# Picking the first expert pair's token rows with TensorE in a two-layer decoder trunk with a routed mixture of experts

## Chip, cores and metric

The kernel is one program on one core of a Trainium2 chip. The metric is the device time of one execution in microseconds (us); smaller is better. All engine times below come from one profiled execution of the kernel before the change.

## What is computed

A residual stream of 272 tokens (16 learned meta tokens ahead of 256 real ones, 1024 features, float32) goes through two layers. Each layer has a mixer (an mLSTM in layer 0, forgetting attention in layer 1, where the meta tokens are dropped) and behind it a mixture of experts, which is the part that the change touches:

```python
def hier_moe(h, w_group, b_group, w_router, b_router, w_gate, w_up, w_down):
    gl = x @ w_group + b_group                     # 4 groups
    top_g = argmax(gl);  p_g = softmax(gl)[top_g]
    el_g = (x @ w_router + b_router)[group top_g]  # 4 experts of that group
    top_v, top_i = top_k(el_g, 2)
    p_e = softmax(top_v) * p_g
    gates = one_hot(eidx) * p_e                    # 16 experts, 2 in use per token
    for grp in range(4):                           # dense in the reference
        act = silu(x @ w_gate) * (x @ w_up) * gates
        y += act @ w_down
    return y
```

with D_MODEL = 1024, 16 experts, an expert width of 256, and 272 tokens in layer 0, 256 in layer 1.

## The kernel before

The code is written per engine: each of SyncE (SP), GpSimd (POOL), ScalarE (ACT), VectorE (DVE) and TensorE (PE) has its own hand-written instruction order, and engines meet at counting semaphores. `in_layer(name, l, n)` is the wait for the n-th increment of a semaphore in layer l.

The expert stage doesn't compute all experts for all tokens. DVE's `route` (from L826) finds two experts for each token and gives each (token, expert) a slot: expert e has 64 slots, two experts form a pair b of 128 slots, and there are 8 pairs. The slot numbers of a token's two experts stand in `tok4[:, 0:2, t]`, for token tiles t = 0, 1 (128 tokens each) and, in layer 0 alone, t = 2 (the 16 meta tokens). The normalised rows of the stream stand in SBUF in `tok` (L589, ACT), and ACT also writes them to DRAM as `xs` (L593).

For pair b the kernel needs the rows of its 128 slots, transposed, in `xgT[b % 2]`. Before the change all eight pairs get them the same way:

- DVE's `one_hot` (L866) and `one_hot_late` (L909) write bf16 one-hot masks `sel` (token x slot).
- PE's `rows_of_slots` (L1369) multiplies them with the token numbers `tcol`, one output column per pair; DVE's `row_of_slot` (L823) makes integers `idx` of it.
- POOL's indirect DMA (L456) gathers the 128 rows of `xs` into `xg[b % 3]`.
- PE's `rows_to_cols` (L1402) transposes them, in two halves of four blocks through `bank[0]`; DVE's `x_evac` (L917) takes the first half out, ACT's `xgT_evac` (L623) the second, both times the norm's gains.

Then for each pair PE runs `gate_up` (L1420, 16 float32 products of 128x512, two column halves of the array at a time), ACT and DVE form silu(gate) x up, PE's `act_tr` (L1427) transposes it, `down` (L1444) and `combine` (L1459 in layer 0, L1463 in layer 1) follow one pair later. A float32 product shows as two MATMUL records, a transpose and a bf16 product as one.

The mixing weights reach the token axis by `tokens_to_rows` (L1382), a copy `row4` (L968), `spread_rows` (L1389) and ACT's `rows_spread` (L615). `keep_busy` (L1349) runs products whose result nobody reads.

Weights stream through a ring of 12 slots of 1 MB (`RING`), filled by SP in a fixed order (L304): six of a pair (gate, up, gate, up, down, down). A gate or up slot is free when the `gate_up` of two pairs earlier is done, a down slot when that pair's `down` is done, and SP waits in order. The first two pairs' weights are loaded while the layer's output projection still runs.

PE's order around the first pair before the change: slot counting, `keep_busy(8)`, `rows_of_slots` of block 0, `keep_busy(18)`, both halves of `rows_to_cols(0)`, `rows_of_slots` of blocks 1 to 3, `tokens_to_rows`, `gate_up(0)`, `spread_rows`, `rows_of_slots` of blocks 4 to 7, `rows_to_cols(1, 0)`, `act_tr(0)`, `rows_to_cols(1, 1)`, `gate_up(1)`, `down(0)`.

Of the kernel before, what the change touches and what calls it, by code (L numbers as in the profile page):

```python
# [11 lines left out]
P = 128  # L12
# [28 lines left out]
def build(nc, io, out):  # L41
    ctx = ExitStack()
    with ctx:
# [56 lines left out]
        comb = big[:, NY * D:NY * D + NPAIR * NT].rearrange("p (b t) -> p b t", t=NT)  # L100
        sel = big[:, 0:6 * 256].bitcast(BF16).rearrange("p (c t s) -> p c t s", c=2, t=3)
# [136 lines left out]
        def wait_bank(pe, kind, ph, j):  # L238
            if before(kind, ph) + j >= 2:
# [7 lines left out]
                  "sel_ready": 5, "idx_mm": 3, "tok4_ready": 1, "row4_mm": 1, "row4_ready": 1, "at_done": 8,  # L247
                  "at_read": 8, "comb_ready": 8, "c_done": 64, "x_in0": 48, "x_in1": 48, "x_in2": 32}
# [131 lines left out]
        def _(pool):  # L380
# [68 lines left out]
            def moe(l):  # L449
                tiles, n, off = tiles_of(l)  # L450
                pool.wait_ge(*in_layer("xs_written", l, 16 * len(tiles)))
                for b in range(NPAIR):
                    pool.wait_ge(*in_layer("idx_ready", l, (1, 2, 2, 2, 3)[min(b, 4)]))
                    if b >= NXG:
                        pool.wait_ge(*in_layer("tx_done", l, 2 * (b - NXG) + 2))
                    pool.indirect_dma_start(  # L456
                        out=xg[b % NXG], out_offset=None, in_=xs[l],
                        in_offset=bass.IndirectOffsetOnAxis(ap=idx[:, b:b + 1], axis=0)) \
                        .then_inc(sem(f"x_in{b % NXG}"), 16)
                pool.wait_ge(*in_layer("ktot_ready", l, 1))  # L460
# [23 lines left out]
        def _(act):  # L484
# [86 lines left out]
            def moe(l):  # L571
# [12 lines left out]
                def rows_out(t, rows):  # L584
# [6 lines left out]
                    link(ins)  # L591
                    r0 = (META, META + P, 0)[t] - off
# [46 lines left out]
                xgT_evac(0)  # L639
# [72 lines left out]
        def _(dve):  # L712
# [113 lines left out]
            def route(l):  # L826
# [8 lines left out]
                t4n, t4bn, dnn, gmn, pgn, exn, dvn = [a[:, 0:nt, :] for a in (t4, t4b, dn, gm, pg, ex, dv)]  # L835
# [43 lines left out]
                one_hot(0, 0, P)  # L879
# [5 lines left out]
                row_of_slot(l, 0, 0, 1, 1)  # L885
                link(dve.tensor_reduce(v12[:, :, 0:nt, 0], t16[:, :, 0:nt, :], AX.X, ALU.add))
                dve.tensor_tensor(dvn, v12[:, 1, 0:nt, :], v12[:, 0, 0:nt, :], ALU.subtract).then_inc(sem("v_sub"), 1)
                one_hot(P, P, 2 * P)
                one_hot(3 * P, 3 * P, P)
# [10 lines left out]
            def moe(l):  # L900
# [64 lines left out]
                x_evac(0)  # L965
                row_of_slot(l, 1, 1, 4, 2)
# [9 lines left out]
                for b in range(NPAIR):  # L976
# [5 lines left out]
                    else:  # L982
                        row_of_slot(l, 3, 4, 8, 3)
                    if b + 1 < NPAIR:
                        x_evac(b + 1)
                    actT_evac(b)
# [189 lines left out]
        def _(pe):  # L1176
# [145 lines left out]
            def moe(l):  # L1322
# [69 lines left out]
                def rows_to_cols(b, half):  # L1392
                    if half == 0:
                        pe.wait_ge(*in_layer(f"x_in{b % NXG}", l, 16 * (b // NXG + 1)))
                        if b >= 1:
                            pe.wait_ge(*in_layer("xT_read", l, b))
                        else:
                            pe.wait_ge(*in_layer("idx_ready", l, 1))
# [6 lines left out]
                def gate_up(b):  # L1405
# [4 lines left out]
                    else:  # L1410
                        pe.wait_ge(*in_layer("idx_ready", l, 2))
# [4 lines left out]
                    for q in range(KB):  # L1416
                        for par in (0, 1):
# [48 lines left out]

                rows_to_cols(0, 0)
                rows_to_cols(0, 1)
                rows_of_slots(3, 1, (1, 2, 3))
                tokens_to_rows()  # L1470
                for b in range(NPAIR):
                    gate_up(b)
                    if b == 0:
                        spread_rows()
                        rows_of_slots(5, 3, (4, 5, 6, 7))
                    if b >= 1:
                        down(b - 1)
                    if b + 1 < NPAIR:
                        rows_to_cols(b + 1, 0)
                    act_tr(b)  # L1480
                    if b >= 1:
                        combine(b - 1, 0)
                    if b + 1 < NPAIR:
# [192 lines left out]
```

## Time and profile before

| | us |
|---|---|
| three timed runs | 687.52, 689.30, 689.37 |
| their median | 689.3 |
| the profiled execution, its own time | 687.83 |
| its span, first to last instruction | 686.1 |
| PE busy | 642.8 (94%) |
| DVE busy | 204.6 (30%) |
| ACT busy | 143.9 (21%) |
| POOL busy | 30.5 (4%) |
| mean granted TensorE clock | 0.972 |

The rows are read as follows. The chain of work that ended last names at each step the instruction that the next one waited for. The timeline lists instructions of each engine in order of time; a neighbouring few of one line are merged (xN), and the time in brackets is idle time before them with what ended it. The views by stretch give busy time, the granted TensorE clock (1.00 is 2.4 GHz, 0.50 is 1.2 GHz) and the busy share of the DMA engines. Durations overlap where an engine pipelines: six instructions of 0.27 us can take 1.25 us together.

### The profile page before, as it was taken

The page shows a single profiled execution, that of the slowest core. Times are in us where ns is not written, and L with a number is a line of the kernel's source. Part 1 is how long each engine was busy: PE and PEld are TensorE (multiplying, and loading weights), DVE is VectorE, ACT ScalarE, POOL GpSimd, SP SyncE. Part 2 cuts the span into 40 slices and gives each one's busy share as a digit, 9 for nine tenths or more (in the row PEclk, how much of TensorE's full clock was granted, in tenths as well). Part 3 has the DMA queues.
Part 4 walks back from the last instruction along what each step waited for, and adds up shares of the span by engine and source line. Part 5 has one row for each costly group of instructions (what it writes and reads, how often), then busy time and mean ns, then how long its engine had stood idle before and what let it go on. Part 6 is the DMA issues. An engine that isn't in the chain of part 4 may idle for free.

```text
span 686.1 us, 7900 instructions
## 1 busy us (share of the span) xinstructions
PE 642.8 (94%) x3052; PEld 399.4 (58%) x3052; DVE 204.6 (30%) x588; ACT 143.9 (21%) x396; POOL 30.5 (4%) x60
## 2 busy tenths in 40 slices
PE   6889999999998999999988999999999889999994
PEld 3577877777674355544446777777677433334331
DVE  2423112222153244444362333333312422112211
ACT  1112012332141011111032333333213211111110
POOL 5000000000002000000001000000000300000000
PEclk9998999999999899999999999999999889999998
DMA  9996232113334599999995504132334376999921
GB/s 289 278 279 216 69 148 88 64 62 122 123 137 140 249 374 415 419 420 416 350 349 177 184 20 166 62 124 67 118 123 155 116 312 274 409 422 419 421 106 63
DMA packets 59114, 150.05 MB, mean 219 GB/s; under 512 B 10082, under 2 KB 42914, under 8 KB 46786
## 3 DMA queue, kind: packets, MB, share of 16 engines
q1 hardware_dynamic: 55554, 136.71, 53.8%
q0 software_dynamic: 2912, 10.64, 4.4%
q10 hardware_dynamic: 608, 2.16, 0.8%
q8 instruction: 26, 0.43, 0.2%
q14 instruction: 14, 0.11, 0.0%
HBM read 146.27 MB, written 3.23 MB: 218 GB/s over the span
## 4 chain that ended last, share of the span: by engine, by line
PE 82%; DMA 8%; ACT 3%; DVE 3%; issue 1%; SPq 1%; ACTq 0%; DVEq 0%
PE bank L1186 34%; PE bank L1420 15%; PE bank L1444 7%; DMA ring<-in_moe_w_up 6%; PE bank L1459 3%; PE bank L1463 3%; PE bank L1281 3%; PE bank L1402 2%; DMA qk_area<-xs,idx 1%; PE bank L1584 1%; PE bank L1195 1%; PE bank L1571 1%; PE bank L1213 1%; PE bank L1613 1%; ACT tok L589 1%
## 5 line engine op out<-in xcount | busy, mean ns | idle before, releaser
L1186 PE MATMUL bank<-xT,ring 128*128 128x272 f32 x640 | 156.8, 401 | 5.2 <-ACT qk_area L523 3.0
L1186 PEld LDWEIGHTS bank<-xT,ring 128*128 128x128 f32 x640 | 122.4, 194 | 32.3 <-issue 6.4
L1420 PE MATMUL bank<-ring,gate_area 128*64 128x512 f32 x512 | 120.8, 627 | 5.9 <-DMA ring<-in_moe_w_up 2.8
L1420 PEld LDWEIGHTS bank<-ring,gate_area 128*64 128x64 f32 x512 | 39.2, 144 | 81.5 <-issue 81.5
L1186 PE MATMUL bank<-tok,ring 128*128 128x272 f32 (+1 forms) x256 | 61.0, 391 | 0.6 <-DVE tok L1170 0.6
L1444 PE MATMUL bank<-ring,gate_area 128*64 128x512 f32 x256 | 57.9, 593 | 0.0
L1186 PEld LDWEIGHTS bank<-tok,ring 128*128 128x128 f32 x256 | 47.4, 190 | 13.5 <-issue 6.1
L936 DVE TENSOR_TENSOR qk_area<-qk_area,bank 128x256 f32<-128x256 f32 x16 | 6.7, 422 | 122.7 <-ACT qk_area L631 122.7
L1444 PEld LDWEIGHTS bank<-ring,gate_area 128*64 128x64 f32 x256 | 19.1, 137 | 35.6 <-issue 35.6
L456 POOL DMA_INDIRECT qk_area<-xs,idx x16 | 18.1, 1129 | 456.7 <-DMA xs<-tok 329.1
L631 ACT ACTIVATE qk_area<-bank 128x256 f32<-128x256 f32 x16 | 6.1, 384 | 131.9 <-PE bank L1420 131.9
L1459 PE MATMUL bank<-big 128*128 128x272 f32 x128 | 32.5, 399 | 1.2 <-DVE big L950 1.2
L1463 PE MATMUL bank<-big 128*128 128x512 f32 x64 | 30.6, 606 | 1.1 <-DVE big L950 1.1
L1402 PEld LDWEIGHTS bank<-ident,qk_area 128*128 128x128 f32 x128 | 18.0, 193 | 20.7 <-issue 12.6
L501 ACT ACTIVATE colT<-hT 128x272 f32<-128x272 f32 (+1 forms) x32 | 13.5, 426 | 76.0 <-DVE hT L818 59.0
L955 DVE TENSOR_TENSOR hT<-hT,bank 128x272 f32<-128x272 f32 x64 | 27.7, 436 | 5.0 <-PE bank L1459 4.1
L1186 PE MATMUL bank<-big,ring 128*128 128x256 f32 x128 | 28.9, 379 | 0.0
L623 ACT ACTIVATE gate_area<-bank,gains_x 128x128 f32<-128x128 f32 x64 | 18.3, 368 | 50.3 <-PE bank L1402 50.3
L1402 PE MATMUL bank<-ident,qk_area 128*128 128x128 f32 x128 | 22.4, 300 | 6.1 <-DMA qk_area<-xs,idx 3.6
L1459 PEld LDWEIGHTS bank<-big 128*128 128x128 f32 x128 | 23.2, 190 | 6.7 <-DVE big L950 2.2
L1186 PEld LDWEIGHTS bank<-big,ring 128*128 128x128 f32 x128 | 24.3, 190 | 3.5
L950 DVE COPY big<-bank 128x512 f32<-128x512 f32 x16 | 11.1, 691 | 45.7 <-PE bank L1444 45.7
(243 smaller groups left out, 593.0 us busy)
## 6 DMA issues: line engine op xcount, KB each, us to landing
ring<-in_moe_w_gate SPq DMA_DIRECT2D x32, 1024.0 KB, 12.3
ring<-in_moe_w_up SPq DMA_DIRECT2D x32, 1024.0 KB, 14.1
ring<-in_moe_w_down SPq DMA_DIRECT2D x32, 1024.0 KB, 7.5
ring<-in_m_w_in SPq DMA_DIRECT2D x12, 1024.0 KB, 11.7
ring<-in_kv_w SPq DMA_DIRECT2D x8, 1024.0 KB, 11.9
ring<-in_m_w_out SPq DMA_DIRECT2D x4, 1024.0 KB, 11.0
ring<-in_f_w_q SPq DMA_DIRECT2D x4, 1024.0 KB, 12.3
ring<-in_f_w_o SPq DMA_DIRECT2D x4, 1024.0 KB, 5.1
```

The costliest lines, as they stand in the source:

```text
L456: pool.indirect_dma_start(out=xg[b % NXG], out_offset=None, in_=xs[l], in_offset=bass.IndirectOffsetOnAxis(ap=idx[:, b:b + 1], axis=0)) \
L501: act.activation(colT[k % 2][:, 0:n], hT[:, k, c0:c0 + n], ACT.Square).then_inc(sem(f"sq_{name}"), 1)
L623: ins = act.activation(xgT[b % 2][:, q, :], bank[0][:, (q - 4) * P:(q - 3) * P], ACT.Copy, scale=gains_x[:, l, q:q + 1])
L950: dve.tensor_copy(yb[b % NY][:, 0:HALF], bank[2][:, :]).then_inc(sem("y_read0"), 1)
L955: dve.tensor_tensor(hT[:, i, :], hT[:, i, :], bank[4 + i % 4][:, 0:NT], ALU.add) \
L1186: ins = pe.matmul(bank[c % 2][:, 0:n], w[:, k, half * P:half * P + P], x[:, k, 0:n], start=(k == 0), stop=(k == KB - 1))
L1281: ins = pe.matmul(bank[b][:, q0:NT], lhs, wexp[0:kr, hd, c:c + NT - q0], start=(m == 0), stop=(m == 2), skip_group_check=True)
L1402: ins = pe.transpose(bank[0][:, i * P:(i + 1) * P], xg[b % NXG][:, 4 * half + i:D:KB], ident[:, :])
L1420: ins = pe.matmul(bank[1][s, :], xgT[b % 2][:, q, s], ring[:, r:r + 2, q * FE:(q + 1) * FE], start=(q == 0), stop=(q == KB - 1))
L1444: ins = pe.matmul(bank[2 + half][s, :], haT[b % 2][:, f, s], unit_down(us[par])[:, f, half * HALF:(half + 1) * HALF], start=(f == 0), stop ...
L1459: ins = pe.matmul(bank[4 + i % 4][:, 0:n], y[:, i * P:(i + 1) * P], comb[:, b, 0:n], start=True, stop=True)
L1463: ins = pe.matmul(bank[4 + i][:, :], comb[:, b, t * P:(t + 1) * P], y[:, half * HALF:(half + 1) * HALF], start=(b == 0), stop=(b == NPAIR ...
```

## The change

For the first pair no gather is made. DVE writes a float32 one-hot mask `sel0` of 128 slots, both experts of a token in one mask (one comparison per tile, then one comparison-and-add per tile). PE's `pick_rows` multiplies the rows in `tok` by it: for each of 8 feature blocks one float32 product per token tile, accumulated, 4 blocks into `bank[0]` and 4 into `bank[1]`. The result is the transposed rows. DVE's `first_evac` takes both halves out; ACT has no part in it. PE waits for `rows_in_sbuf` (the rows of all tiles written by ACT) and `sel0_ready`.

The rest is order:

- The slot's token numbers are worked out in parts: block 1 ahead of `gate_up(0)`, blocks 2 and 3 and `tokens_to_rows` in the middle of it (behind its fourth of eight steps), blocks 4 to 7 behind it. POOL gathers pair 1 after the first part, 2 and 3 after the second, the others after the third.
- `keep_busy(18)` is gone, `keep_busy(8)` is `keep_busy(10)`.
- The six small DVE operations on the mixing weights (`gate_weights`) are moved out of `route`, behind `first_evac` and the first `row_of_slot`.
- Behind `gate_up(0)` PE's order becomes `rows_to_cols(1, 0)`, `spread_rows`, `rows_to_cols(1, 1)`, `rows_of_slots` of blocks 4 to 7, `act_tr(0)`, `gate_up(1)`. On DVE `x_evac(1)` comes ahead of `row_of_slot` of the last blocks.

```diff
-                for b in range(NPAIR):
-                    pool.wait_ge(*in_layer("idx_ready", l, (1, 2, 2, 2, 3)[min(b, 4)]))
+                for b in range(1, NPAIR):
+                    pool.wait_ge(*in_layer("idx_ready", l, min(b // 2, 2) + 1))
...
                     link(ins)
+                    act.sem_inc(sem("rows_in_sbuf"), 1)
...
-                xgT_evac(0)
...
-                one_hot(0, 0, P)
+                for t, rows, _ in tiles:
+                    ins = dve.tensor_scalar(sel0[0:rows, t, :], iota_f[0:rows, 0:P], tok4[0:rows, 0, t:t + 1], None,
+                                            ALU.is_equal)
+                link(ins)
+                for t, rows, _ in tiles:
+                    ins = dve.scalar_tensor_tensor(sel0[0:rows, t, :], iota_f[0:rows, 0:P], tok4[0:rows, 1, t:t + 1],
+                                                   sel0[0:rows, t, :], ALU.is_equal, ALU.add)
+                ins.then_inc(sem("sel0_ready"), 1)
+                one_hot(P, P, P)
...
-                row_of_slot(l, 0, 0, 1, 1)
...
-                one_hot(P, P, 2 * P)
-                one_hot(3 * P, 3 * P, P)
+                one_hot(2 * P, 2 * P, 2 * P)
+            def gate_weights(l):
...
+                def first_evac(half):
+                    dve.wait_ge(*in_layer("tx_done", l, half + 1))
+                    q = slice(4 * half, 4 * half + 4)
+                    dve.tensor_tensor(xgT[0][:, q, :], bank[half][:, :].rearrange("p (q s) -> p q s", q=4),
+                                      gains_x[:, l, q].unsqueeze(2).to_broadcast([P, 4, P]), ALU.mult) \
+                        .then_inc(sem(("xT_read0", "xT_read")[half]), 1)
...
-                x_evac(0)
-                row_of_slot(l, 1, 1, 4, 2)
+                first_evac(0)
+                first_evac(1)
+                row_of_slot(l, 0, 1, 2, 1)
+                gate_weights(l)
+                row_of_slot(l, 0, 2, 4, 2)
...
-                keep_busy(8)
-                if l == 0:
-                    pe.wait_ge(*in_layer("xr_read", l, 1))
-                rows_of_slots(1, 0, (0,))
-                keep_busy(18)
+                keep_busy(10)
+                def pick_rows(half):
+                    for i in range(4):
+                        for m, (t, rows, _) in enumerate(tiles):
+                            ins = pe.matmul(bank[half][:, i * P:(i + 1) * P], tok[0:rows, t, 4 * half + i:D:KB],
+                                            sel0[0:rows, t, :], start=(m == 0), stop=(m == nt - 1))
+                    ins.then_inc(sem("tx_done"), 1)
...
                     for q in range(KB):
+                        if b == 0 and q == KB // 2:
+                            pe.wait_ge(*in_layer("idx_ready", l, 1))
+                            rows_of_slots(2, 0, (2, 3))
+                            tokens_to_rows()
...
-                rows_to_cols(0, 0)
-                rows_to_cols(0, 1)
-                rows_of_slots(3, 1, (1, 2, 3))
-                tokens_to_rows()
+                pe.wait_ge(*in_layer("rows_in_sbuf", l, nt))
+                pe.wait_ge(*in_layer("sel0_ready", l, 1))
+                pick_rows(0)
+                pick_rows(1)
+                pe.wait_ge(*in_layer("xT_read0", l, 1))
+                rows_of_slots(1, 0, (1,))
                 for b in range(NPAIR):
                     gate_up(b)
-                    if b == 0:
-                        spread_rows()
-                        rows_of_slots(5, 3, (4, 5, 6, 7))
                     if b >= 1:
                         down(b - 1)
                     if b + 1 < NPAIR:
                         rows_to_cols(b + 1, 0)
+                    if b == 0:
+                        spread_rows()
+                        rows_to_cols(1, 1)
+                        rows_of_slots(4, 3, (4, 5, 6, 7))
                     act_tr(b)
```

## Rows read from the trace of the kernel before

**Rows 1.** Page, the chain that ended last, shares of the span by engine

```profile
PE 82%; DMA 8%; ACT 3%; DVE 3%; issue 1%; SPq 1%; ACTq 0%; DVEq 0%
```

**Rows 2.** The chain in order of time: start us, us, what, both layers

```profile
203.03 4.70 DMA qk_area<-xs,idx
...
211.95 8.29 PE bank L1420 x32
...
228.02 8.82 PE bank L1420 x32
...
542.43 8.63 PE bank L1420 x32
...
556.79 9.97 PE bank L1420 x32
```

**Rows 3.** Timeline of ACT and DVE, layer 0: start us, us, engine, instruction

```profile
199.20 1.25 ACT L589 ACTIVATE tok<-bank,rs 16x512 f32<-16x512 f32 x2 [0.40 <-ACT tok L589]
...
199.66 0.26 DVE L878 TENSOR_REDUCE tok<-gate_area 128x6 f32<-128x96 f32 x1
199.96 1.25 DVE L866 TENSOR_SCALAR big<-iota_f,tok 128x128 bf16<-128x128 f32 x6
...
202.43 3.06 DVE L866 TENSOR_SCALAR big<-iota_f,tok 128x256 bf16<-128x256 f32 x12
...
208.52 0.69 DVE L917 TENSOR_TENSOR gate_area<-bank,gains_x 128x512 f32<-128x512 f32 x1 [1.94 <-PE bank L1402]
...
225.81 0.49 DVE L925 SCALAR_TENSOR_TENSOR gate_area<-gate_area,s_cols 128x272 f32<-128x272 f32 x1
```

**Rows 4.** Timeline of PE, layer 0, from the routing on, and a later gate

```profile
201.82 4.29 PE L1349 MATMUL bank<-ident,ones_f 128*128 128x128 f32 x36
...
207.77 0.71 PE L1402 MATMUL bank<-ident,qk_area 128*128 128x128 f32 x4 [1.66 <-DMA qk_area<-xs,idx]
...
209.81 1.50 PE L1369 MATMUL bank<-tcol,big 128*128 128x1 bf16 x18
...
211.25 0.70 PE L1382 MATMUL bank<-ident,tok 128*4 128x128 f32 x3
...
220.17 2.10 PE L1389 MATMUL bank<-colT,sel 4*128 4x272 f32 x8
...
222.20 1.99 PE L1369 MATMUL bank<-tcol,big 128*128 128x1 bf16 x24
...
293.20 7.09 PE L1420 MATMUL bank<-ring,gate_area 128*64 128x512 f32 x32 [0.91 <-DMA ring<-in_moe_w_up]
```

**Rows 5.** Timeline of PE and DVE, layer 1

```profile
529.85 2.03 PE L1349 MATMUL bank<-ident,ones_f 128*128 128x128 f32 x16
...
530.81 0.22 DVE L878 TENSOR_REDUCE tok<-gate_area 128x4 f32<-128x64 f32 x1
...
552.91 0.55 PE L1369 MATMUL bank<-tcol,big 128*128 128x1 bf16 x16
```

**Rows 6.** Line L1402: weight loads, duration ns min/median/max, first and last start

```profile
L1402 PEld LDWEIGHTS bank<-ident,qk_area x128: 185/190/231, 207.8 to 652.0; 128*128 128x128 f32 x128
```

**Rows 7.** Groups by shape, 201.7 to 206.2 us: busy us, mean ns, idle before

```profile
L1349 PEld LDWEIGHTS bank<-ident,ones_f 128*128 128x128 f32 x36 | 4.1, 192 | 0.0
```

**Rows 8.** Busy by stretch: us, PE busy (x), granted clock, DMA share, GB/s

```profile
211.00:214.60 3.60, 3.60 (x15) 0.53 0.18 40
...
224.70:228.00 3.30, 1.68 (x8) 0.50 0.98 412
...
556.80:562.60 5.80, 5.80 (x14) 0.50 1.02 425
```

**Rows 9.** SP's waits, 195 to 345: us in total, times, longest

```profile
SPq L304 <- PE bank L1444: 82.8, 6, 17.9
```

**Rows 10.** One steady pair: us, busy PE, PEld, DVE, ACT, POOL, clock, DMA

```profile
255.88:271.50 15.62, 15.62 (x76) 7.51 (x75) 6.72 (x15) 2.13 (x6) 0.94 (x1) 1.00 1.01 414
```

**Rows 11.** Line L456, the 16 gathers: time from issue to landing

```profile
DMA to landing us min/median/max: 4.6/6.4/10.2
```

More of the change, by code:

```diff
@@ L100, in build @@
         comb = big[:, NY * D:NY * D + NPAIR * NT].rearrange("p (b t) -> p b t", t=NT)
+        sel0 = big[:, 6 * 256:6 * 256 + 3 * P].rearrange("p (t s) -> p t s", t=3)
         sel = big[:, 0:6 * 256].bitcast(BF16).rearrange("p (c t s) -> p c t s", c=2, t=3)
@@ L246, in build @@
                   "act_ready": 8, "down_done": 8, "y_read0": 8, "y_read1": 8, "eall_ready": 1, "pos_mm": 1,
-                  "sel_ready": 5, "idx_mm": 3, "tok4_ready": 1, "row4_mm": 1, "row4_ready": 1, "at_done": 8,
-                  "at_read": 8, "comb_ready": 8, "c_done": 64, "x_in0": 48, "x_in1": 48, "x_in2": 32}
+                  "sel_ready": 4, "idx_mm": 3, "tok4_ready": 1, "row4_mm": 1, "row4_ready": 1, "at_done": 8,
+                  "at_read": 8, "comb_ready": 8, "c_done": 64, "sel0_ready": 1, "rows_in_sbuf": 3, "x_in0": 32, "x_in1": 48, "x_in2": 32}
         def in_layer(name, l, n):
@@ L834, in route @@
                 gl, el = lg[:, 0:nt, 0:NG], lg[:, 0:nt, NG:NG + NE]
-                t4n, t4bn, dnn, gmn, pgn, exn, dvn = [a[:, 0:nt, :] for a in (t4, t4b, dn, gm, pg, ex, dv)]
+                t4n, gmn, dvn = [a[:, 0:nt, :] for a in (t4, gm, dv)]
                 ogb = og[:, 0:nt, :].unsqueeze(3).to_broadcast(full)
@@ L884, in route @@
                 link(dve.tensor_tensor(t16[:, :, 0:nt, :], el.unsqueeze(1).to_broadcast(both), e12[:, :, 0:nt, :], ALU.mult))
-                row_of_slot(l, 0, 0, 1, 1)
                 link(dve.tensor_reduce(v12[:, :, 0:nt, 0], t16[:, :, 0:nt, :], AX.X, ALU.add))
                 dve.tensor_tensor(dvn, v12[:, 1, 0:nt, :], v12[:, 0, 0:nt, :], ALU.subtract).then_inc(sem("v_sub"), 1)
-                one_hot(P, P, 2 * P)
-                one_hot(3 * P, 3 * P, P)
+                one_hot(2 * P, 2 * P, 2 * P)
+            def gate_weights(l):
+                tiles, n, off = tiles_of(l)
+                nt = len(tiles)
+                t4bn, dnn, pgn, exn = [a[:, 0:nt, :] for a in (t4b, dn, pg, ex)]
                 dve.wait_ge(*in_layer("gl_exp", l, 1))
@@ L981, in moe @@
                         y_evac(b - 1)
-                    else:
-                        row_of_slot(l, 3, 4, 8, 3)
                     if b + 1 < NPAIR:
                         x_evac(b + 1)
+                    if b == 0:
+                        row_of_slot(l, 3, 4, 8, 3)
                     actT_evac(b)
@@ L1393, in rows_to_cols @@
                     if half == 0:
[L1394 to L1398, printed above, removed]
+                        pe.wait_ge(*in_layer(f"x_in{b % NXG}", l, 16 * (b // NXG + (b % NXG > 0))))
+                        pe.wait_ge(*in_layer("xT_read", l, b))
+                        if b == 1:
+                            pe.wait_ge(*in_layer("idx_ready", l, 2))
                     else:
@@ L1409, in gate_up @@
                         pe.wait_ge(*in_layer("at_read", l, b))
-                    else:
-                        pe.wait_ge(*in_layer("idx_ready", l, 2))
                     us = [expert_units(l, b, par) for par in (0, 1)]
@@ L1479, in moe @@
                         rows_to_cols(b + 1, 0)
+                    if b == 0:
+                        spread_rows()
+                        rows_to_cols(1, 1)
+                        rows_of_slots(4, 3, (4, 5, 6, 7))
                     act_tr(b)
@@ L1482, in moe @@
                         combine(b - 1, 0)
-                    if b + 1 < NPAIR:
+                    if 1 <= b < NPAIR - 1:
                         rows_to_cols(b + 1, 1)
```

## The prediction, made blind

> **What bounds the kernel now.** I read the chain that ended last first: it is TensorE for 82% of the span and DMA for 8% [rows 1]. Anything that the change gives must therefore be found on PE's own path or in what PE waits for. The chain in order of time then says where the first expert pair stands: in layer 0 it leaves PE for the gather (203.03, 4.70 us) and comes back at the transposes, and the first gate stage runs from 211.95 for 8.29 us, the second from 228.02 for 8.82 us; in layer 1 they start at 542.43 and 556.79 and last 8.63 and 9.97 us [rows 2]. A later one, from 293.20, lasts 7.09 us [rows 4]. So each layer holds two things: a detour (mask, token numbers, gather, transposes, two evacuations) and early gate stages that are slower than the later ones. The view by stretch names the reason for the second: the clock was at 0.50 to 0.53, that is at 1.2 GHz, in 211 to 214.6, in 224.7 to 228, and in 556.8 to 562.6 [rows 8]. Before each fall PE had run transposes and one-column products and been idle in between; it came back while gate products ran.
>
> Behind the second gate stage everything is tied to PE. SP's longest waits, six of them, are for L1444, the down stage [rows 9], so the weight stream starts again from there. In a steady pair PE is busy all of its 15.62 us and the DMA engines are too (1.01, 414 GB/s) [rows 10]. Both shift together if the first `down` comes earlier.
>
> **Layer 0, up to the first gate stage.** The slots are known at 199.66 + 0.26 = 199.92 [rows 3]. The mask `sel0` takes three comparisons and three comparison-adds of 128 columns. Six comparisons take 1.25 us with 0.27 for the first alone, so 0.20 each behind it [rows 3]; for the comparison-add no row has this size: a 272-column one takes 0.49 [rows 3], a comparison 0.27, and I take 0.30 and 0.22 for each further one. Sum 0.67 + 0.74 + 0.05 for the link = 1.46, so `sel0` is ready at 201.4. ACT's last row is there at 200.45 [rows 3] and doesn't decide; PE's ten idle products (20 records at 0.12) end near 201.2.
>
> `pick_rows` is the new cost, and its price is the main unknown. It is 2 x 4 x 3 = 24 float32 products, 48 records. The nearest row is `keep_busy`: 36 records of the same moving shape in 4.29 us, 0.119 each [rows 4]. The other bound is the transposes from the same kind of strided operand: 4 records in 0.71; with the last one's 0.28 taken off, 0.14 to 0.15 between starts [rows 4]. I take 0.12, as a load over the stride lasts as long (median 190 ns) as one of `ones_f` (mean 192) [rows 6, 7]; 0.147 would add 80 x 0.027 = 2.2 us over both layers. So 48 x 0.12 + 0.16 = 5.9 us, end at 207.4. One evacuation (0.69 [rows 3]) is hidden beside the second half, DVE being through its masks at about 205.6 (201.4 + 1.25 + 1.15 for five small steps + 3.06 - 1.25 for the wide ones [rows 3]); the other stands on the path. The first gate stage starts at 207.4 + 0.05 + 0.69 = 208.2, against 211.9: **3.7 us** sooner. The six one-column products of block 1 (0.5 us at 1.50/18 [rows 4]) lie beside that evacuation.
>
> The stride has a rule against it. The Trainium skill, SBUF — State Buffer, in its note on cachelines, says that reads which step to a new 16-byte line each time pay a penalty; `tok[..., i:D:8]` steps 32 bytes. The trace doesn't agree (190 beside 192 ns). The page gives no figure; by the rule the sum would go toward its upper bound.
>
> **Layer 0, first gate stage to second.** Two pieces move into the stage: 12 one-column products, 12 x 1.50/18 = 1.0, and `tokens_to_rows`, 0.63 [rows 4]. At full clock the stage is 7.1 + 1.6 = 8.7 and ends at 216.9 (220.2 before). The added wait there, for `idx_ready`, holds nothing: DVE writes that column at 208.4, four steps take until 211.8. Behind it: `rows_to_cols(1,0)` 0.7, `spread_rows` 2.0, second half 0.7, 24 one-column products 2.0 [rows 4], `act_tr` 0.5 and its copy 0.5, in all 6.4, so `gate_up(1)` starts at 223.3. ACT's evacuation of pair 1 (1.14, some 220.6 to 221.8) is now beside the one-column products, where it used to be last. Against 228.02: **4.7 us**.
>
> The masks for blocks 4 to 7 start on DVE only when `row4` is copied, at 214.1, and take 3.2, so they end at 217.3; their reader comes at 220.3. The six `gate_weights` steps (1.2 us) lie between 208.5 and 211.9, where DVE has nothing else. POOL's first gather is issued near 208.7 and lands 4.7 to 10.2 us later [rows 2, 11]; it is wanted at 216.9, so there are 8.2 us for it, and it is alone on the queue. The later gathers keep their order.
>
> **Layer 1** has two tiles. Slots at 531.03 [rows 5], `sel0` at 532.1; PE's idle products, from 529.85 [rows 5], end at 532.3 and decide. 32 records: 3.84 + 0.16, end at 536.3; evacuation, start at 537.1 against 542.43: 5.3 us. The stage takes 7.05 + 0.35 + 0.5 = 7.9 (the one-column products are 0.55/16 each here [rows 5]); then 0.7 + 2.0 + 0.7 + 0.55 + 0.5 + 0.5 = 5.0. Second gate stage at 550.1 against 556.79: **6.7 us**.
>
> **The clock in the second gate stage.** It cost 8.82 - 7.09 = 1.73 us in layer 0 and 9.97 - 7.09 = 2.88 in layer 1 [rows 2, 4]. After the change the quiet stretch behind `spread_rows` is 3.6 us instead of 5.8, and 2.1 instead of 3.8. Real products fill the place where gather waits stood, so the first gate stage should run at full clock (already in the sums). For the second I can't say: bounds for what is left are 0 and the old cost; I take 1.3 in each, so the change gives back 1.73 + 2.88 - 2.6 = **2.0 us**.
>
> Here one rule bears. In the Trainium skill, TensorE: Matmul & The Clock Gate, Part 4, transposes are said not to count as busy for the clock. The low clock from 224.7 and at 556.8 [rows 8] came behind one-column products and transposes, which agrees. By that rule the quiet stretch lasts up to the gate stage and the clock still falls; if transposes did count, it might not, which is the rival of 672.4 below.
>
> **Sum:** 4.7 + 6.7 + 2.0 = 13.4. From the profiled execution, 687.8 - 13.4 = 674.4; from the median of 689.3 it would be 675.9. I take 675.0.
>
> **Rivals.**
> - *The weight stream decides.* It starts again first at the end of `gate_up(0)`, which moves by only 3.3 and 5.9 us. If PE later waits for weights as before (0.91 us ahead of the stage at 293.20 [rows 4], and alike in layer 1) and that wait grows by the rest, 687.8 - 9.2 = 678.6. For it speaks the full DMA share; against it that the six long waits are for `down` [rows 9], which moves in full.
> - *The gather of pair 1 lands late.* At 10.2 us it comes 2.0 us late in layer 0 and, issued at 537.6 and wanted at 545.0, 2.8 late in layer 1: 674.4 + 4.8 = 679.2. Against it: a single gather took 4.70.
> - *The clock falls before the picks*, as PE waits for `sel0`. Each record then takes twice as long: 80 x 0.12 = 9.6 more, 684.0. The idle time is only 0.3 us, far less than what lay ahead of the falls [rows 8].
> - *The clock never falls:* 674.4 - 2.6 = 671.8 from this execution, 672.4 from the middle of both starts.
> - *Slower.* The picks don't pipeline because each product loads its own strided weights: load and product behind one another, 0.19 + 0.28 = 0.47 per record. 80 x 0.35 = 28 more, 702. It decides from 0.12 + 13.4/80 = 0.29 per record. `keep_busy` has loads of 0.192 and still starts a record each 0.119 [rows 4, 7].
> - *It doesn't do what it says:* the wait goes elsewhere in front of `gate_up(0)`, 687.8. DVE would have to be the late one by 4 us; its queue holds no such thing.
>
> **How the numbers follow.** The forecast 0.60, weight stream 0.12, late gather 0.10, clock low in the picks 0.06, clock never low 0.08, slower 0.02, no effect 0.02. The forecast's own ends are 672.5 (old clock cost gone in one layer) and 679 (0.147 per record, no clock gain). The range 671.0 to 680.5 takes in all but about 0.15. A difference of 0.3% (2 us) is about what a measurement of this kernel can tell from none; by these cases faster 0.96, same 0.02, slower 0.02.
>
> **What would show it.** Right: no idle PE at L1402 for a gather in front of the first gate stage; the picks 48 and 32 records in 5.9 and 4.0 us at clock 1.00; the first gate stage starting 8.3 us behind the slot reduction in layer 0 and 6.3 in layer 1; the gap between the first two gate stages 6.4 and 5.0; 15.6 us per pair behind it as before. Wrong: picks spaced over 0.15 us, a clock of 0.50 within them, a new wait for `qk_area<-xs,idx` before pair 1, DVE still at its masks when the first half is picked, or PE's waits for weights up by more than 1 us.

## The result, and the profile after

The changed kernel takes 692.3 us (median of 14 runs, 690.2 to 697.1) where the kernel before takes 689.2 (14 runs, 685.9 to 690.6): ratio 1.005, 95% interval 1.0034 to 1.0067. It is slower by half a per cent, and the interval leaves out 1, where 675.0 us and a range of 671.0 to 680.5 had been forecast. The profiled execution took 692.3 us with a span of 690.6, 4.5 us more than the 686.1 of before.

**The chain.** By engine, from the page of the kernel after, to be read beside [rows 1]:

```profile
PE 86%; DMA 6%; DVE 3%; ACT 2%; issue 1%; SPq 1%; DVEq 0%; ACTq 0%
```

The gather is off the chain, as the change intends (DMA 6% for 8%), and PE has taken more than its place. The chain in order of time (start us, us, what), layer 0 and then layer 1, says with what:

```profile
201.63 16.00 PE bank L1404 x48
218.46 4.99 PE bank L1450 x16
223.45 0.96 PE bank L1394 x12
...
224.83 3.58 PE bank L1450 x16
...
235.13 8.62 PE bank L1450 x32
...
540.03 7.86 PE bank L1404 x32
...
548.72 5.35 PE bank L1450 x16
554.59 3.58 PE bank L1450 x16
...
562.78 8.64 PE bank L1450 x32
```

L1404 is `pick_rows`, L1450 is `gate_up`. The picks take 16.00 and 7.86 us, forecast at 5.9 and 4.0. The first gate stage starts at 218.46 where it had started at 211.95 [rows 2].

**The picks themselves.** One line's instructions (duration ns min/median/max, first and last start, shapes), kernel after, beside [rows 6, 7] with their 190 and 192:

```profile
L1404 PEld LDWEIGHTS bank<-big,tok x80: 307/335/340, 201.6 to 547.4; 128*128 128x128 f32 x64, 16*128 16x128 f32 x16
L1404 PE MATMUL bank<-big,tok x80: 396/439/607, 201.6 to 547.5; 128*128 128x128 f32 x64, 16*128 16x128 f32 x16
```

Each weight load takes 335 ns. And the clock, by stretch (us, PE busy (x), granted clock, DMA share, GB/s), kernel after:

```profile
201.63:204.00 2.37, 2.37 (x9) 1.00 0.07 19
204.00:205.00 1.00, 1.00 (x4) 0.57 0.00 0
205.00:217.60 12.60, 12.60 (x39) 0.50 0.00 0
218.46:221.00 2.54, 2.54 (x6) 0.50 0.00 0
540.03:547.50 7.47, 7.47 (x32) 1.00 0.11 42
549.00:552.00 3.00, 3.00 (x8) 0.50 0.25 70
```

In layer 0 the clock falls to its lower level (1.2 GHz) in the midst of the picks, while PE shows no idle time, and stays there into the first gate stage. (In front of them it had been idle for 0.45 us, waiting for `sel0`.) In layer 1 the picks run at 1.00 from end to end, 7.86/32 = 0.25 us each, and the clock falls just behind them.

**Where the 4.5 us are.** At the end of layer 0's second gate stage the kernel is 243.75 - 236.84 = 6.9 us behind. PE's wait for a weight, 0.91 us before [rows 4], is 1.67, which with the rest of layer 0 makes layer 1's share start 7.7 late (slots known at 538.50 against 530.81 [rows 5]). Timeline of PE, kernel after, that stage (the row stops where the view was cut off):

```profile
300.87 4.51 PE L1450 MATMUL bank<-ring,gate_area 128*64 128x512 f32 x20 [1.67 <-DMA ring<-in_moe_w_up]
```

Timeline of DVE, kernel after, where layer 1's slots are known:

```profile
538.50 0.22 DVE L879 TENSOR_REDUCE tok<-gate_area 128x4 f32<-128x64 f32 x1
```

Layer 1 gives 3.0 back: its second gate stage ends at 571.42, which less 7.7 is 563.7, where it was 566.8 before. 6.9 + 0.8 - 3.0 is 4.7; the 4.5 of the spans leave 0.2 for what comes behind. So layer 1, with two tiles and an undisturbed clock in its picks, is a gain even at the double price, and layer 0 is a loss.

### The profile page after: what moved, and what is told of

Read it like the earlier page. It is cut to its first block, busy times and chain, and to the rows that moved or that the text cites. A ratio compares the mean times of both kernels' runs of the same rounds, so it can differ in the third digit from the quotient of the medians.

```text
span 690.6 us, 7878 instructions
## 1 busy us (share of the span) xinstructions
PE 653.8 (95%) x3042; PEld 409.5 (59%) x3042; DVE 206.3 (30%) x590; ACT 141.6 (21%) x388; POOL 28.6 (4%) x58
## 4 chain that ended last, share of the span: by engine, by line
PE 86%; DMA 6%; DVE 3%; ACT 2%; issue 1%; SPq 1%; DVEq 0%; ACTq 0%
PE bank L1211 33%; PE bank L1450 15%; PE bank L1474 7%; DMA ring<-in_moe_w_up 6%; PE bank L1404 3%; PE bank L1489 3%; PE bank L1493 3%; PE bank L1306 3%; PE bank L1430 2%; PE bank L1617 1%; PE bank L1220 1%; PE bank L1604 1%; PE bank L1238 1%; PE bank L1646 1%; PE bank L1342 1%
## 5 line engine op out<-in xcount | busy, mean ns | idle before, releaser
L1450 PE MATMUL bank<-ring,gate_area 128*64 128x512 f32 x512 | 120.0, 621 | 5.8 <-DMA ring<-in_moe_w_up 3.4
L1450 PEld LDWEIGHTS bank<-ring,gate_area 128*64 128x64 f32 x512 | 38.9, 143 | 78.8 <-issue 78.8
L457 POOL DMA_INDIRECT qk_area<-xs,idx x14 | 16.2, 1155 | 462.6 <-DVE idx L824 371.6
L1430 PEld LDWEIGHTS bank<-ident,qk_area 128*128 128x128 f32 x112 | 15.5, 192 | 15.4 <-issue 14.9
L1404 PE MATMUL bank<-big,tok 128*128 128x128 f32 (+1 forms) x80 | 23.9, 453 | 0.5 <-DVE big L886 0.5
L625 ACT ACTIVATE gate_area<-bank,gains_x 128x128 f32<-128x128 f32 x56 | 16.0, 368 | 32.6 <-PE bank L1430 32.6
```

What stands on the lines that cost most here:

```text
L457: pool.indirect_dma_start(out=xg[b % NXG], out_offset=None, in_=xs[l], in_offset=bass.IndirectOffsetOnAxis(ap=idx[:, b:b + 1], axis=0)) \
L625: ins = act.activation(xgT[b % 2][:, q, :], bank[0][:, (q - 4) * P:(q - 3) * P], ACT.Copy, scale=gains_x[:, l, q:q + 1])
L1404: ins = pe.matmul(bank[half][:, i * P:(i + 1) * P], tok[0:rows, t, 4 * half + i:D:KB], sel0[0:rows, t, :], start=(m == 0), stop=(m == nt - 1))
L1430: ins = pe.transpose(bank[0][:, i * P:(i + 1) * P], xg[b % NXG][:, 4 * half + i:D:KB], ident[:, :])
L1450: ins = pe.matmul(bank[1][s, :], xgT[b % 2][:, q, s], ring[:, r:r + 2, q * FE:(q + 1) * FE], start=(q == 0), stop=(q == KB - 1))
```

## The experiments

My first theory was that the stride of the picks' weights costs the time: `tok[..., i:D:8]` takes every eighth float32 of a row. Its rivals: float32 products with new weights in each cost that much in any layout; the clock alone; the new order behind the picks. Each ratio below is to the kernel before, timed together with the experiment. Where a time is that of a single execution, it proves little by itself, and only durations within it are compared.

**1. The same picks without the stride.**

```diff
-    ins = pe.matmul(bank[half][:, i * P:(i + 1) * P], tok[0:rows, t, 4 * half + i:D:KB],
+    ins = pe.matmul(bank[half][:, i * P:(i + 1) * P], tok[0:rows, t, (4 * half + i) * P:(4 * half + i + 1) * P],
```

> The kernel after with one thing changed: the weights that the picks load are 128 neighbouring features of a row instead of every eighth one. The experts of the first pair then get features in another order, so this kernel computes something else for that pair; its amount of work is the same. Theory A (the stride makes each weight load long): loads back from 335 to about 190 ns, layer 1's 32 records from 7.9 to about 3.9 us, layer 0's 48 records from 16.0 to about 5.8 us with the clock at 1.00 throughout, and the whole at about 678 us. Theory B (a float32 product with these two operands is slow whatever the stride): loads stay at 335 ns and layer 1 at 7.9 us, the whole stays at 692 us. Theory C (only the fallen clock costs): layer 1, where the clock stayed at 1.00, doesn't change.

681.2 us, ratio 0.9863 (0.9816 to 0.9911), where the changed kernel has 1.005. The line of the picks, the chain and the clock in them, this kernel:

```profile
L1404 PEld LDWEIGHTS bank<-big,tok x80: 181/192/192, 202.3 to 538.0; 128*128 128x128 f32 x64, 16*128 16x128 f32 x16
```

```profile
202.31 8.48 PE bank L1404 x48
211.62 5.35 PE bank L1450 x16
...
534.62 3.81 PE bank L1404 x32
```

```profile
202.31:210.60 8.29, 8.29 (x48) 1.00 0.02 4
```

The edit changes one access pattern and nothing else, and takes 11 us away. Layer 1's picks cost 3.81 us, 0.119 a record, the forecast's own price; the clock held within the picks in both layers. Layer 0's still cost 8.48 for 48 records, 0.177 each, so something is left there: see 5. Behind them the first half of the gate stage still took 5.35 us in layer 0, where it takes 3.65 at full clock.

**2. At which stride it begins.** The same line with every second and every fourth feature (8 and 16 bytes between elements) instead of every eighth (32 bytes).

> As before but every second feature (8 bytes between elements). The rule of 16-byte lines in the Trainium skill (SBUF - State Buffer, note on cachelines) has two elements in a line and no or a small penalty: loads near 190 ns. If instead any step costs: 335 ns.

> As before but every fourth feature (16 bytes between elements, one element to a line). By the rule of 16-byte lines the full penalty of the kernel after, 335 ns per load; if the cost goes with the number of bytes stepped over, about halfway between 190 and 335 ns.

679.0 and 695.1 us in a single execution each. The picks' loads with every second, then with every fourth feature:

```profile
L1404 PEld LDWEIGHTS bank<-big,tok x80: 187/196/197, 200.4 to 533.6; 128*128 128x128 f32 x64, 16*128 16x128 f32 x16
```

```profile
L1404 PEld LDWEIGHTS bank<-big,tok x80: 303/330/330, 204.2 to 550.2; 128*128 128x128 f32 x64, 16*128 16x128 f32 x16
```

4, 8, 16 and 32 bytes give 192, 196, 330 and 335 ns: a step between 8 and 16 bytes, and nearly no slope at either side. So the price doesn't grow with the distance; it fits a price for loads of which no two elements share 16 bytes. (Steps of 12 bytes and other starts within the 16 were not run.) The Trainium skill, SBUF — State Buffer, asks in Specifications (TRN2) for two or more hits to each 16-byte line; the runs agree with that for these loads. It is the rule that the prediction had set aside.

**3. Product or transpose.** The row I had set it aside on was a transpose's. The kernel before, with only the first pair's eight turnings written as float32 products with the identity, on the same gathered buffer with the same stride:

```diff
-    ins = pe.transpose(bank[0][:, i * P:(i + 1) * P], xg[b % NXG][:, 4 * half + i:D:KB], ident[:, :])
+    src = xg[b % NXG][:, 4 * half + i:D:KB]
+    if b == 0:
+        ins = pe.matmul(bank[0][:, i * P:(i + 1) * P], src, ident[:, :], start=True, stop=True)
+    else:
+        ins = pe.transpose(bank[0][:, i * P:(i + 1) * P], src, ident[:, :])
```

> The kernel before with one thing changed: the first pair's gathered rows are turned by float32 products with the identity instead of transposes, from the same gathered buffer with the same stride of eight. If float32 products load their weights slower over a stride and transposes don't, the loads go from 190 to 335 ns here too, 16 records instead of 8. If the rows' own buffer in the kernel after is the cause, they stay at 190 ns. The whole: 1 to 4 us slower than before at most.

692.4 us in a single execution. Groups by shape in 200 to 213 us (busy us, mean ns, idle before), this kernel:

```profile
L1404 PEld LDWEIGHTS bank<-ident,qk_area 128*128 128x128 f32 x16 | 4.0, 334 | 2.7 <-DMA qk_area<-xs,idx 1.8 <-DVE gate_area L917 1.0
```

334 ns as a product, 190 as a transpose [rows 6], same buffer, same stride, same shape. The row of the transposes was a true one and said nothing of a product's loads.

**4. The layout made contiguous with the right output.** ACT writes the normalised rows block by block, and the picks, the transposes and the later use of `xg` read 128 neighbours.

```diff
+    by_block = tok[0:rows, t, :].rearrange("r (k p) -> r p k", k=KB)
...
-    ins = act.activation(tok[0:rows, t, half * HALF:(half + 1) * HALF], b[0:rows, :], ACT.Copy,
+    ins = act.activation(by_block[:, half * 64:(half + 1) * 64, :],
+                         b[0:rows, :].rearrange("r (p k) -> r p k", k=KB), ACT.Copy,
```

> The kernel after, computing what the reference asks, with the feature order changed: ACT writes each normalised row block by block (feature 8p + i to column 128i + p), so every weight load of the picks and of the transposes of the gathered rows reads neighbouring elements. Stride theory: the picks as with stride 1, 48 records in about 8.5 us and 32 in 3.8, the whole near 681 us. Against it: ACT's copies write 512 bytes apart; if they slow down from 0.64 to 1 us each, the mask waits for rows and the whole loses 2 to 3 us, 683.

> The kernel before with the blocked feature order alone, first pair still gathered. Transposes already loaded in 190 ns over the stride, so the order alone should be worth nothing: 689 us, within 0.3%. If it were worth several us, the gain of after_blocked over before would not be the picks'.

The changed kernel with it: 688.1 us, ratio 0.9977 (0.9955 to 0.9999). The kernel before with the layout alone: 695.1, ratio 1.008 (1.0048 to 1.0112), which I had put at nothing. ACT's copies (timeline of ACT) in the kernel before and then in the second of these:

```profile
195.84 1.27 ACT L589 ACTIVATE tok<-bank,rs 128x512 f32<-128x512 f32 x2
```

```profile
194.36 2.06 ACT L590 ACTIVATE tok<-bank,rs 128x512 f32<-128x512 f32 x2
```

The price has moved to the writer: 0.8 us for each tile, in front of the gather or the picks. In the kernel before with this layout that is not all of the loss: in layer 1 the write of the rows to DRAM, on which the gather waits, lands 4.53 us after its issue where it took 2.65, and no run says why. In the changed kernel with it, PE waits for the copies, and the clock falls in the picks though their loads are cheap. Groups by shape in 198 to 220 us, and by stretch:

```profile
L1406 PE MATMUL bank<-big,tok 128*128 128x128 f32 x32 | 8.9, 427 | 1.8 <-ACTq L595 1.8
L1406 PE MATMUL bank<-big,tok 16*128 16x128 f32 x16 | 6.0, 475 | 0.0
```

```profile
205.00:217.50 12.50, 12.50 (x44) 0.50 0.00 0
```

The 48 records take 13.9 us here and 8.5 in 1, with the same operands: the low clock alone costs 5.4. In layer 1 they take 3.84. So the fall in the picks isn't the stride's doing alone: it came with cheap loads behind an idle time of 1.8 us, and with dear loads behind one of 0.5.

**5. What is left in layer 0: the 16 meta rows.** There each block of picks is three products, over 128, 128 and 16 rows. Two theories: a record over 16 rows is dear by itself; or the change between loads of 128 and of 16 rows is. Kernel 1 again, the third product over 128 rows of tile 0:

```diff
-    ins = pe.matmul(bank[half][:, i * P:(i + 1) * P], tok[0:rows, t, (4 * half + i) * P:(4 * half + i + 1) * P],
-                    sel0[0:rows, t, :], start=(m == 0), stop=(m == nt - 1))
+    u = t % 2
+    ins = pe.matmul(bank[half][:, i * P:(i + 1) * P], tok[:, u, (4 * half + i) * P:(4 * half + i + 1) * P],
+                    sel0[:, u, :], start=(m == 0), stop=(m == nt - 1))
```

> As pick_stride1, and in layer 0 the third product of each block reads tile 0 with 128 rows again instead of the meta tokens' 16 rows; so it computes something else for the first pair, with the same number of records. Theory E (records over 16 rows cost about twice those over 128): layer 0's 48 records take 5.8 us instead of 8.5. If three accumulated products cost that in themselves: 8.5 us as before.

676.9 us in a single execution. Timeline of PE, this kernel:

```profile
200.36 5.60 PE L1405 MATMUL bank<-big,tok 128*128 128x128 f32 x48 [0.45 <-DVE big L886]
```

More rows in the array, and 2.9 us less. To tell the two theories apart I took kernel 4 and put all 16-row products of a half behind the others. This kernel doesn't compute what the reference asks for the first pair; the amount of work is the same.

```diff
-    for i in range(4):
-        for m, (t, rows, _) in enumerate(tiles):
+    blocks = [(i, m) for i in range(4) for m in range(min(nt, 2))] + [(i, 2) for i in range(4) if nt == 3]
+    for i, m in blocks:
+        t, rows, _ = tiles[m]
...
```

> As after_blocked, and in layer 0 the products over the 16 rows of meta tokens come last in each half instead of every third. With stride 1 layer 0's picks took 0.177 us a record where layer 1's took 0.119. Theory D (changing between 128 and 16 rows of weights breaks the overlap of load and product): layer 0's 48 records drop from 8.5 toward 5.8 us, the whole by 2 to 3 us to about 678.5. Theory E (a load over 16 rows is slow wherever it stands): no change.

681.7 us, ratio 0.9876 (0.9841 to 0.9911); the picks took 9.38 us, not the 5.8 that grouping would give if the change of height were the cost. I first read that as the end of that theory, and it was a misreading: the low clock fell into this stretch too. By stretch, and the loads of the last group on their own (timeline of weight loads), this kernel:

```profile
205.00:210.00 5.00, 5.00 (x23) 0.50 0.00 0
211.40:212.20 0.80, 0.80 (x7) 1.00 0.00 0
```

```profile
211.32 0.96 PEld L1407 LDWEIGHTS bank<-big,tok 16*128 16x128 f32 x8 [0.22 <-issue]
```

Back at full clock, eight 16-row loads stand in 0.96 us, 0.12 each: as cheap as 128 rows. Another kernel separates the two at full clock. It is kernel 1 with every second block in reverse order (128, 128, 16, then 16, 128, 128), so that the sums hold and the height changes 8 times instead of 15:

```diff
-    for m, (t, rows, _) in enumerate(tiles):
+    for m, (t, rows, _) in enumerate(tiles[::(1, -1)[i % 2]]):
```

> The kernel after with the picks at stride 1 (each block takes 128 neighbouring features instead of every eighth, so the columns of the first pair's rows stand in another order, as in pick_stride1), and every second block takes its tiles in reverse (128, 128, 16, then 16, 128, 128 rows), so that the 48 records of layer 0 change between 128 and 16 rows 8 times instead of 15. At stride 1 and full clock a record starts 0.112 us behind the one before; the records at a change cost some 0.1 more each, and the 48 took 8.48 us where all of 128 rows took 5.60. Theory CHANGE (what costs is the change of height between one product's weights and the next's, 2.88 us / 15 = 0.19 each): the picks of layer 0 take 5.6 + 8 x 0.19 = 7.1 us, layer 1's stay at 3.81, the 16-row records in the middle of a run of four start 0.112 apart, and the time is about 1.4 us below that of pick_stride1, 679.9. Theory HEIGHT (a record over 16 rows is dearer by itself, 0.18 more for each of the 16): the picks stay at 8.5 us and the time at 681.2.

679.2 us, ratio 0.9837 (0.9778 to 0.9895). Timeline of PE, this kernel:

```profile
204.28 7.14 PE L1404 MATMUL bank<-big,tok 128*128 128x128 f32 x48 [0.45 <-DVE big L886]
```

7.14 us where the change of height gives 7.1 and a price of the height itself 8.5. The starts of the records within one and a half blocks show it singly; ns from each record to the next, 16-row records in brackets:

```
every eighth feature, clock 1.00 (after)           239 238 331 [340 326] 339
every eighth feature, clock 0.50 (after)           238 242 378 [399 370] 400
neighbours, clock 1.00 (pick_stride1)              112 112 205 [213 200] 213 112
neighbours, clock 1.00 (pick_stride1_turned)       112 112 205 [213 112 111 200] 214 111
neighbours, clock 0.50 (after_blocked)             213 214 350 [375 347] 374 213
```

At full clock each change of height costs two records some 0.09 to 0.10 us more, at the lower one 0.13 to 0.16. And a record over the stride takes 238 to 242 ns at either clock: the lower clock costs it nothing by itself, only at the changes.

**6. The rest of the change without the picks.** Pair 0 gathered and transposed as before, with its token numbers and `keep_busy` of before; the parts of the other token numbers, the moved weight steps and the new order kept. One thing is neither before nor after: PE waits for block 1's numbers (`idx_ready`) in front of the first gate stage, where the changed kernel waits for them in its middle.

```diff
-    pe.wait_ge(*in_layer("sel0_ready", l, 1))
-    pick_rows(0)
-    pick_rows(1)
+    rows_to_cols(0, 0)
+    rows_to_cols(0, 1)
...
+    pe.wait_ge(*in_layer("idx_ready", l, 2))
```

> The kernel after with the picks undone: the first pair's rows are gathered and transposed as before, all the rest is in the new order (block 1's numbers ahead of the first gate stage, blocks 2 and 3 and the mixing weights' transposes inside it, the new sequence behind it). From the traces the gap between the first two gate stages shrank from 7.8 to 6.7 and from 5.7 to 4.6 us: so 2 us faster than before, 687, if the order brings what the traces suggest; the moved pieces lengthen the first gate stage by what they left out in front of it, nothing either way. Rival: it brings up to 4 us, as fewer one-column products stand in front of the first gate stage.

690.1 us, ratio 1.0021 (0.9998 to 1.0044): not the 687 that I had put, and no gain. Timeline of PE, this kernel:

```profile
211.83 5.88 PE L1450 MATMUL bank<-ring,gate_area 128*64 128x512 f32 x16 [0.98 <-DVE idx L825]
...
229.17 3.68 PE L1450 MATMUL bank<-ring,gate_area 128*64 128x512 f32 x8 [0.67 <-issue]
```

The first half of the gate stage takes 5.88 us, at a clock of 0.61, where before it took 4.8 (16 records from 211.88 to 216.64), and the inserts lengthen the stage by 1.3. The gap behind it shrinks from 7.8 to 6.5 us, which doesn't pay for that: the second gate stage starts 2.3 us later than before, both measured from the masks' start. Of these 2.3 us about 1.0 is this kernel's own wait for `idx` in front of the stage, which the changed kernel doesn't have. So the run shows no gain of the order behind a gather; what the order is worth behind quick picks was not run by itself.

**7. Select first, then turn.** The mask as the stationary operand and 512 contiguous features moving; ACT copies each half to `xg[0]`, and eight strided transposes turn it. Transposes don't pay for the stride, and neither do products over neighbours. Two idle products (`keep_busy(2)`) stand between the selection and the transposes.

```diff
-    for i in range(4):
-        for m, (t, rows, _) in enumerate(tiles):
-            ins = pe.matmul(bank[half][:, i * P:(i + 1) * P], tok[0:rows, t, 4 * half + i:D:KB],
-                            sel0[0:rows, t, :], start=(m == 0), stop=(m == nt - 1))
+    for m, (t, rows, _) in enumerate(tiles):
+        ins = pe.matmul(bank[half][:, :], sel0[0:rows, t, :], tok[0:rows, t, half * HALF:(half + 1) * HALF],
+                        start=(m == 0), stop=(m == nt - 1))
...
+    act.activation(xg[0][:, half * HALF:(half + 1) * HALF], bank[half][:, :], ACT.Copy)
...
+    ins = pe.transpose(bank[half][:, i * P:(i + 1) * P], xg[0][:, 4 * half + i:D:KB], ident[:, :])
```

> The kernel after, computing what the reference asks, with the first pair's rows selected the other way round: the mask is the stationary operand (contiguous) and the rows the moving one, 512 features at a time (6 products in layer 0, 4 in layer 1, 0.44 us each at full clock), ACT copies both halves to the gather's buffer, and 8 transposes over the stride (190 ns loads) turn them as before. If the picks' price in the kernel after is the strided weight load of float32 products, this pays none of it: 2.7 + 1.3 for the copy behind + 1.2 us in layer 0 instead of 16.0, 1.8 + 1.3 + 1.2 in layer 1 instead of 7.9. Whole: 690.6 - 10.8 - 3.6 gives about 677 to 680 us with the clock as it falls. If something else of the change costs the time (order, DVE's masks, the missing idle products), it stays above 686.

679.5 us, ratio 0.9855 (0.9818 to 0.9891), and it computes what the reference asks: it beats both kernels. Timeline of PE, this kernel, layer 0:

```profile
204.16 5.97 PE L1407 MATMUL bank<-tok,big 128*128 128x512 f32 x12 [0.45 <-DVE big L890]
210.06 0.71 PE L1378 MATMUL bank<-ident,ones_f 128*128 128x128 f32 x4
210.82 1.17 PE L1414 MATMUL bank<-ident,qk_area 128*128 128x128 f32 x8
...
212.96 3.65 PE L1459 MATMUL bank<-ring,gate_area 128*64 128x512 f32 x16
```

I had put the selection at 2.7 us; it took 5.97, as a full-width product is two records of about 0.5 us each and I had counted one. In layer 1 the second gate stage ran at full clock from start to end (7.09 us), as in no other kernel of this study; why there isn't known:

```profile
550.66 7.09 PE L1459 MATMUL bank<-ring,gate_area 128*64 128x512 f32 x32 [0.67 <-ACT gate_area L629]
```

**8. The forecast's own case.** The first kernel of 5 (neighbouring features, no product over 16 rows), whose picks cost what the forecast had taken for them, timed against the kernel before.

> The kernel of pick_stride1_full, now timed against the kernel before: picks over neighbouring features and no product over 16 rows, so that they cost what the prediction put them at (5.6 us for 48 records in layer 0 in the look before, forecast 5.9), and all else as in the kernel after. It computes something else for the first pair. If the price of the picks was the one thing wrong in the prediction, this comes to 675 to 677 us, a ratio of 0.979 to 0.983. If the order or the other moves carry a loss of their own, it stays above 679.

676.5 us, ratio 0.9806 (0.9746 to 0.9865); the profiled execution took 677.0. The chain in order of time, this kernel:

```profile
200.50 5.60 PE bank L1405 x48
...
206.93 3.65 PE bank L1452 x16
...
222.02 9.36 PE bank L1452 x32
...
349.36 5.51 PE bank L1596 x16
...
528.68 3.81 PE bank L1405 x32
533.32 3.65 PE bank L1452 x16
...
545.98 9.52 PE bank L1452 x32
```

With the one disputed price put right, the kernel comes out 2.6 us from the sum (677.0 against 674.4 for a profiled execution). Part of that closeness is luck, as errors of both signs stand behind it: see the next section.

## Why the prediction was wrong

**The failed step is the price of a pick.** The sum had 80 records at 0.12, with 0.147 as the upper bound. They took 16.00 + 7.86 = 23.9 us instead of 9.9. Split by the runs, layer 0's 10.4 us over the 5.60 of kernel 8 are: the stride, 48 x (0.238 - 0.112) = 6.0; the changes of height, 8.48 - 5.60 = 2.9; and 1.5 left for the low clock at those changes. Layer 1's 7.86 - 3.81 = 4.05 are the stride alone.

**Both bounds came from rows of other work.** `keep_busy` [rows 7] reads contiguous weights of one height; the transposes [rows 6] read over the stride but are no products. The price lay in the combination, a product that reads its weights over a stride, which neither row has, and in the change of height, which neither has either. The upper bound wasn't one: by the order of the argument, the rule against the stride should have been given its own rival, with a load that decides the spacing, and it was dismissed on a transpose's load instead. The height of the weights was not weighed at all, though a row had a sign of it: L1369 takes 1.50 us for 18 one-column records in layer 0, six of them over 16 rows [rows 4], and 0.55 for 16 in layer 1 [rows 5]. The `slower` rival had the right side by another mechanism. Picks do pipeline (loads of 335 ns, starts every 238); the spacing came out at 0.33 and 0.25 us, about the 0.29 from which it was to decide, and the result lies as near to no change as that says.

**The clock in the picks** was put at 6 in 100, on the ground that PE's idle time ahead of them is short (0.3 us). It was (0.45 us), and in layer 0 the clock fell all the same. It did so too in the kernel with every fourth feature (15.78 us) and in the two blocked ones behind 1.8 us of idle time; it held in the six others (experiments 1, 2 with every second feature, both forms of 5 on kernel 1, 7 and 8), and in all of layer 1's picks. What sets it off is open.

**The first gate stages** were to run at full clock, 8.7 and 7.9 us. They took 9.95 and 9.46, at 0.50 at their start, 2.8 us more. Behind kernel 8's quick picks they ran at full rate (3.65 for the first half), so this comes with the slow picks. How is not shown: in layer 0 the first half took 5.35 us behind 8.48 us of picks in kernel 1, and 3.65 behind 8.79 in the kernel with every second feature.

**What held.** `sel0` ready at 201.5 (201.4 forecast). But for the 0.45 us for `sel0` there is no PE wait for a gather or for DVE in front of pair 1: `first_evac` waits for the picks, not they for it. The gaps between the first two gate stages were 6.7 and 4.6 us (6.4 and 5.0). In kernel 8 the first gate stage starts 8.2 and 6.0 us behind the end of the slot reduction (8.3 and 6.1 by the forecast's sums; its 6.3 for layer 1 counts from the reduction's start), and the second one 4.8 and 7.1 us sooner than before, by the same mark (4.7 and 6.7). Weights stayed in time there: the wait that was 0.91 us is 0.94, and PE's three waits for weights together are 3.2 us against 2.8.

**One more term was wrong and hidden by the large one:** the 2.0 us that the clock was to give back in the second gate stages. In kernel 8 they take 9.36 and 9.52 us against 8.82 and 9.97, no gain in the sum; the clock starts at 0.50 in both. Another 1.7 us went to a low clock far away, in layer 1's front (349.36, 5.51 us, where the kernels before and after have 3.83). Against these 3.8 us stand 1.2 by which layer 0's slots were known earlier than in the kernel before, ahead of anything that the change touches. That leaves 2.6 us, by which kernel 8's profiled execution (677.0) misses 674.4; picks that are 0.5 us cheaper than forecast and 0.4 us more waiting for weights about cancel.

**A slip in the range.** The forecast's own lower end, 672.5, is said to come from the old clock cost gone in one layer. With 1.3 us left in the other it comes to 674.4 - 1.3 = 673.1. Nothing else hangs on it.

**In one sum:** from 674.4 to the 692.3 of the profiled execution are 17.9 us: 14.0 for the picks, 2.8 for the clock in the first gate stages, 0.8 for the weights and the rest of layer 0, and 0.3 for the gaps, the second gate stages and the tail together.

## What to carry to other kernels

Take the price of a new operation from a row that has the same operation, the same access pattern and the same number of rows; where none has all three, the rows at hand don't bound it, and a rule that names the pattern deserves a rival of its own. For the order of magnitude: here the pattern of access took 0.126 us a record, the height 0.19 us a change. When weights must be read over a stride, let a transpose do it and let the products read neighbours; keep products of different height in runs. Read the granted clock of each stretch before a difference in its duration is put down to anything else: a fall of the clock in one experiment all but buried the right theory on the 16-row records.

## What the runs showed that I had not expected

- Weight loads of float32 products of 128 columns: 192, 196, 330, 335 ns at 4, 8, 16, 32 bytes from element to element; transposes over 32 bytes 190.
- The load over the stride sets the pace at either clock: records every 238 to 242 ns at 1.00 and at 0.50, where neighbours give 112 and 213.
- A change between weights of 128 and of 16 rows costs two records about 0.1 us each more at full clock; 16-row weights among themselves cost what 128 rows cost.
- ACT's copy of 128x512 float32 out of PSUM takes 1.03 us when its consecutive elements are written 512 bytes apart and 0.64 when it writes neighbours.
- The clock fell to 0.50 within a stretch of float32 products in which PE shows no idle time: 2.5 us into the picks of layer 0, behind 0.45 us of idle time.
